# Up products of the recurrent stage as three single-pass products each, on one Trainium2 core

## The reference, cut to what matters

```python
def trunk_layer(x, ...):
    u = rmsnorm(x, g_mix) @ w_in
    u_rw, u_ml, u_pool, u_gate = jnp.split(u, IN_SPLITS, axis=-1)
    o_rw, ... = rwkv7_mix(u_rw, ...)      # 16 heads x 64, recurrent
    o_ml, ... = mlstm_mix(u_ml, ...)
    o_pool, ... = pool_mix(u_pool, ...)
    g = sigmoid(u_gate).reshape(B, L, 3, D_MODEL)
    merged = (g[:, :, 0] * (o_rw @ w_up_rwkv) + g[:, :, 1] * (o_ml @ w_up_mlstm)
              + g[:, :, 2] * (o_pool @ w_up_pool))
    x = x + merged @ w_out
    ...                                    # cross attention, then a mixture of experts
```

## Time and profile before

| | us |
|---|---|
| median of 3 runs (lowest, highest) | 1915.89 (1915.38, 1916.56) |
| the profiled execution, its own time | 1918.07 |
| its span, first to last instruction | 1916.1 |
| PE busy in the span | 1748.7 (91%) |
| DVE, ACT, POOL busy in the span | 910.2, 604.8, 270.5 |
| mean granted TensorE clock (1 is 2.4 GHz) | 0.960 |

### The profile page before, as it was taken

One profiled execution on the slowest core, in us unless ns is written; L12 is line 12 of the kernel. 1 busy time (PEld: TensorE's weight loads), 2 busy tenths in 40 slices (PEclk: granted clock), 3 DMA queues, 4 the chain that ended last, 5 costly groups with the idle time before them and its releaser, 6 DMA issues. The chain is left out here.

```text
span 1916.1 us, 36779 instructions
## 1 busy us (share of the span) xinstructions
PE 1748.7 (91%) x14891; PEld 1439.4 (75%) x14891; DVE 910.2 (48%) x1610; ACT 604.8 (32%) x890; POOL 270.5 (14%) x286
## 2 busy tenths in 40 slices
PE   7999999999999999999998999999898868777675
PEld 7999899998787778778777999999796434443242
DVE  6553445555756676576665445455423222121223
ACT  5243223333443344344335333335432101110012
POOL 0550003112010100100010000850050000000002
PEclk9999999999999999999998999999998988898888
DMA  7445353434232223233215446455638999999995
GB/s 270 174 155 187 110 179 117 173 135 167 100 112 90 99 101 122 87 112 112 90 55 204 155 175 250 152 220 214 238 159 338 422 431 432 431 431 431 431 431 248
DMA packets 46600, 408.98 MB, mean 213 GB/s; under 512 B 6580, under 2 KB 8376, under 8 KB 16696
## 3 DMA queue, kind: packets, MB, share of 16 engines
q1 hardware_dynamic: 46520, 407.81, 54.2%
HBM read 396.62 MB, written 11.18 MB: 213 GB/s over the span
## 5 line engine op out<-in xcount | busy, mean ns | idle before, releaser
L387 PE MATMUL ps<-x_high,w_high 128*128 128x288 f32 x928 | 257.4, 303 | 9.3 <-ACT w_high L593 9.3
L388 PE MATMUL ps<-x_rest,w_high 128*128 128x288 f32 x928 | 253.1, 299 | 0.0
L387 PEld LDWEIGHTS ps<-x_high,w_high 128*128 128x128 f32 x928 | 177.1, 191 | 12.8 <-ACT w_high L593 10.2
L388 PEld LDWEIGHTS ps<-x_rest,w_high 128*128 128x128 f32 x928 | 177.1, 191 | 0.5
L549 ACT ACTIVATE w_high<-w_raw 128x2048 fp32r<-128x2048 f32 x57 | 109.2, 1915 | 153.9 <-DMA w_raw<-in_w_main 77.5
L1101 PE MATMUL ps<-x_high,r_high 128*128 128x288 f32 x512 | 145.8, 308 | 3.8 <-ACT r_high L1352 3.8
L660 DVE TENSOR_TENSOR w_rest<-w_raw,w_high 128x2048 fp32r<-128x2048 f32 x58 | 137.1, 2369 | 11.0 <-ACT w_high L549 11.0
L2557 PE MATMUL ps<-half_a,xg 128*32 128x512 f32 x240 | 81.4, 840 | 62.3 <-DMA half_b<-in_w_egu 62.0
L1101 PE MATMUL ps<-rx_low,r_high 128*128 128x288 f32 x480 | 134.7, 305 | 0.0
L392 PE MATMUL ps<-x_high,w_rest 128*128 128x288 f32 x928 | 132.1, 295 | 1.0 <-DVE w_rest L660 1.0
L392 PEld LDWEIGHTS ps<-x_high,w_rest 128*128 128x128 f32 x928 | 126.0, 188 | 1.2 <-DVE w_rest L660 1.2
(11 more groups left out here) (600 smaller groups left out, 3824.1 us busy)
## 6 DMA issues: line engine op xcount, KB each, us to landing
w_raw<-in_w_main SPq DMA_DIRECT2D x57, 1024.0 KB, 4.8
ring<-in_w_g SPq DMA_DIRECT2D x32, 1024.0 KB, 4.8
half_a<-in_w_egu SPq DMA_DIRECT2D x15, 2048.0 KB, 18.0
half_b<-in_w_egu SPq DMA_DIRECT2D x15, 2048.0 KB, 22.3
ring<-in_w_u SPq DMA_DIRECT2D x32, 512.0 KB, 4.2
ring<-in_w_gate SPq DMA_DIRECT2D x8, 2048.0 KB, 7.8
ring<-in_w_out SPq DMA_DIRECT2D x8, 2048.0 KB, 7.8
half_d<-in_w_egu SPq DMA_DIRECT2D x8, 2048.0 KB, 20.7
```

Source lines behind the costliest of these rows:

```text
L387: mm(o, high[:, t % 2, k, :], x_h[:, k, :], start=(k == 0), stop=False)
L388: ins = mm(o, high[:, t % 2, k, :], x_l[:, k, :], start=False, stop=False)
```

## The change

1. The up products become three single-pass products each, like the gates: up group product numbers run to 24. Products 0 to 15 are high weights by high and low inputs, 16 to 23 the weights' rests by the high inputs. ACT makes the high part of an up tile (`up`, step `j..`, 128x1024, into one buffer `up_high`), POOL its rests (`rest`, step `r..`, 128x1024, into the tile's place). PE waits for `j..` ahead of product 0 and for `r..` ahead of product 16. `j..` waits until the tile before has been read by PE (step `V..`) and by POOL. For `U01`, `U10`, `U11` both are made in the same lap, for `U00` at the end of the lap before.
2. `o_ml` and `o_pool` are split once, in the front stage: ACT rounds (`outcome_high`, and a second scaled copy of the pooling outputs), POOL subtracts (`outcome_rest`, and one operation over all of `o_pool`). The first up tile is split there too, at the stage's end. DVE does `o3` ahead of the last tile's evacuation, and the last tile's rest earlier.
3. The fillers are laid anew. ACT's second half of `split("11")` moves from the fourth level to behind `sas` (with a wait on PE in `G11`, step `i11`), DVE's second half of `rest("11")` behind `s0`. SP waits for `l11` too ahead of one load in the last lap.
4. The last lap of ACT and POOL is written out behind the loop, since it has no tile for a next lap. `bc` moves into another tensor; the scratch for descriptors shrinks from 1024 to 256.

```diff
--- before.py
+++ after.py
+            with ExitStack() as split:
+                sb("o_room", [P, 2 * KH, T], split)
+                o_h, o_l = rounded("o_high", [P, 2 * KH, T], "o_room"), rounded("o_rest", [P, 2 * KH, T], "o_ml")
+                with ExitStack() as c:
+                    front = sb("front", [P, FRONT], c)
+                    up_h, up_rest = rounded("up_high", [P, KH, P], "front"), rounded("up_rest", [P, 2, KH, P], "ring", 6144)
+                    stage_front(nc, ctx, A, O, locals())
+                stage_rwkv(nc, ctx, A, O, locals())
...
+            def outcome_high(h):
+                act.wait_ge(*((g_.sem, g_.at(f"o{h}")) if h < MLH - 1 else (v.sem, v.at("o3"))))
+                fn(o_h[:, 2 * h:2 * h + 2, :], o_ml[:, 2 * h:2 * h + 2, :], ACT.Copy).then_inc(o_high, 1)
...
-                        ins = fn(o_pool[:, 2 * h + e, :], ps[:, 4 + e, 0:T], ACT.Copy, scale=par("pool_scale", 2 * h + e))
+                        by = par("pool_scale", 2 * h + e)
+                        fn(o_pool[:, 2 * h + e, :], ps[:, 4 + e, 0:T], ACT.Copy, scale=by)
+                        ins = fn(o_h[:, KH + 2 * h + e, :], ps[:, 4 + e, 0:T], ACT.Copy, scale=by)
...
+                if h >= 2:
+                    outcome_high(h - 2)
...
+            outcome_high(MLH - 2)
+            outcome_high(MLH - 1)
+            act.wait_ge(env["up_slots"][0], 16)
+            act.wait_ge(q.sem, q.at(f"dB{MLH - 1}"))
+            fn(up_h[:, :, :], up_raw, ACT.Copy).then_inc(up_high, 1)
...
-                step(t + 7)
+                if h < MLH - 1:
+                    step(t + 7)
+            rest(TILES - 1)
             inverse_of(MLH - 1)
-            evacuate(TILES - 1)
+            evacuate(TILES - 2)
             dve.wait_ge(g_.sem, g_.at(f"y{MLH - 1}"))
             dve.wait_ge(v.sem, v.at(f"rs{MLH - 1}"))
             v.done(finish(tt, MLH - 1), "o3")
+            evacuate(TILES - 1)
 
         @block.gpsimd
...
+            tt(o_l[:, KH:2 * KH, :], o_pool[:, :, :], o_h[:, KH:2 * KH, :], ALU.subtract)
...
+            def outcome_rest(h):
+                pool.wait_ge(o_high, h + 1)
+                tt(o_l[:, 2 * h:2 * h + 2, :], o_ml[:, 2 * h:2 * h + 2, :], o_h[:, 2 * h:2 * h + 2, :], ALU.subtract)
...
+                if h:
+                    outcome_rest(h - 1)
             gated(MLH - 1)
+            outcome_rest(MLH - 2)
+            outcome_rest(MLH - 1)
+            pool.wait_ge(up_high, 1)
+            tt(up_rest[:, 0, :, :], up_raw, up_h[:, :, :], ALU.subtract)
...
+            sp.wait_ge(v.sem, v.at("l11", N - 1))
...
                     if kind == "U":
+                        of = i - 1 if name == "U00" else i
                         if lo == 0:
-                            pe.wait_ge(up_slots[b], i * 32 + 16 * d + 16)
+                            pe.wait_ge(a.sem, a.at("j" + name[1:], of))
                             pe.wait_ge(v.sem, v.at(f"m1{b}", i - 1) if d == 0 else v.at(("wm0", "su1")[b], i))
+                        o = ps[:, (1, 7)[b], 0:T]
                         for t in range(lo, hi):
-                            src = (o_ml, o_pool)[b]
-                            ins = mm(ps[:, (1, 7)[b], 0:T], w_up[:, b, t, :], src[:, t, :], start=(t == 0), stop=(t == KH - 1))
-                        if hi == KH:
+                            k = t // 2 if t < 2 * KH else t - 2 * KH
+                            if t < 2 * KH:
+                                ins = mm(o, up_h[:, k, :], (o_h, o_l)[t % 2][:, KH * b + k, :], start=(t == 0), stop=False)
+                                if t == 2 * KH - 1:
+                                    q.done(ins, "V" + name[1:])
+                                continue
+                            if k == 0:
+                                pe.wait_ge(g_.sem, g_.at("r" + name[1:], of))
+                            ins = mm(o, up_rest[:, b, k, :], o_h[:, KH * b + k, :], start=False, stop=(k == KH - 1))
+                        if hi == 3 * KH:
                             q.done(ins, name)
                         return
                     o = ps[:, 6 if name == "G01" else 0, 0:T]
...
+                        if name == "G11" and t == KD:
+                            pe.wait_ge(a.sem, a.at("i11", i))
...
-                filler("U00", 0, 8)
-                filler("U01", 0, 4)
+                filler("U00", 0, 24)
+                filler("U01", 0, 20)
...
                 filler("G00", 0, 48)
-                filler("U01", 4, 8)
+                filler("U01", 20, 24)
                 filler("G01", 0, 48)
...
                 filler("G10", 17, 22)
                 back(1)
-                filler("G10", 22, 32)
+                filler("G10", 22, 31)
                 forward(2)
-                filler("U10", 0, 2)
+                filler("U10", 0, 7)
                 back(2)
                 sample("sz0", lambda h: sxm[:, 0, h, :], lambda h: ident_s)
-                filler("U10", 2, 4)
+                filler("U10", 7, 14)
                 forward(3)
-                filler("U10", 4, 6)
+                filler("U10", 14, 16)
+                filler("G10", 31, 36)
                 back(3)
                 sample("sz1", lambda h: sxm[:, 1, h, :], lambda h: st_[:, h, :])
-                filler("U10", 6, 8)
+                filler("G10", 36, 43)
                 forward(4)
-                filler("G10", 32, 40)
+                filler("G10", 43, 48)
+                filler("U10", 16, 18)
                 back(4)
                 sample("su1", lambda h: sz[:, h, :], lambda h: su[:, h, :])
-                filler("G10", 40, 48)
+                filler("U10", 18, 24)
...
                 q.done(ins, "z5")
-                filler("U11", 0, 2)
+                filler("U11", 0, 6)
...
                 q.done(ins, "u5")
-                filler("U11", 2, 4)
+                filler("U11", 6, 12)
                 q.done(ins, "z6")
-                filler("U11", 4, 6)
+                filler("U11", 12, 18)
                 q.done(ins, "u6")
-                filler("U11", 6, 8)
+                filler("U11", 18, 24)
...
+            def turn(i, last=False):
...
+                def up(name, of):
+                    n = order.index(name)
+                    act.wait_ge(up_slots[n % 2], of * 32 + 16 * (n // 2) + 16)
+                    act.wait_ge(q.sem, q.at("V" + order[n - 1], i))
+                    act.wait_ge(g_.sem, g_.at("r" + order[n - 1], i - 1 if n == 1 else i))
+                    a.done(fn(up_h[:, :, :], w_up[:, n % 2, :, :], ACT.Copy), "j" + name)
...
+                up("01", i)
                 split("00")
...
                 split("10")
+                up("10", i)
...
-                        split("11", 8, 16)
+                        up("11", i)
...
                 a.done(fn(tok[upper, 2, 0:P], ps[upper, 5, P:2 * P], ACT.Copy, scale=-1.0), "sas")
+                split("11", 8, 16)
                 act.wait_ge(q.sem, q.at("g1", i))
...
+                if last:
+                    a.left_out(act, "j00", i)
+                else:
+                    up("00", i + 1)
...
-                rest("11", 8, 16)
                 WQ("s0")
                 halves = [slice(64 * h, 64 * h + 64) for h in H]
                 for o in halves:
                     ins = ts(st0[o, o], ps[o, 2, 0:64], er[o, P - 1:P], ec[o, 1:2], ALU.mult, ALU.mult)
                 v.done(ins, "s0")
+                rest("11", 8, 16)
                 WQ("s1")
...
+                def rest(name):
+                    b = int(name[1])
+                    g_.done(tt(up_rest[:, b, :, :], w_up[:, b, :, :], up_h[:, :, :], ALU.subtract), "r" + name)
+                pool.wait_ge(a.sem, a.at("j01", i))
+                rest("01")
...
+                pool.wait_ge(a.sem, a.at("j10", i))
+                rest("10")
                 pool.wait_ge(v.sem, v.at("m01", i))
                 m = mrg[:, bass.ds(i * 2, 1), :].rearrange("p o t -> p (o t)")
                 g_.done(tt(m, m, gtmp[:, :], ALU.add), "m0")
+                pool.wait_ge(a.sem, a.at("j11", i))
+                rest("11")
                 pool.wait_ge(a.sem, a.at("sas", i))
                 g_.done(spread(vnx[:, :, :], tok[0:2 * NSM, 2, 0:P]), "nx")
+                if last:
+                    g_.left_out(pool, "r00", i)
+                else:
+                    pool.wait_ge(a.sem, a.at("j00", i))
+                    rest("00")
                 pool.wait_ge(v.sem, v.at("m11", i))
                 m = mrg[:, bass.ds(i * 2 + 1, 1), :].rearrange("p o t -> p (o t)")
```

More of the change, by code:

```diff
@@ L212, in stage_front @@
         SUM_AFTER, SLOTS = 4, 3
-        x_h, x_l = env["x_h"], env["x_l"]
+        x_h, x_l, o_h, o_l, up_h, up_rest = (env[n] for n in "x_h x_l o_h o_l up_h up_rest".split())
         raw, w_rest = placed("w_raw", [P, SLOTS, KD, P], "ring"), rounded("w_rest", [P, SLOTS, KD, P], "ring")
@@ L247, in stage_front @@
         whole = ring[:, :, :].rearrange("p s n -> p (s n)")
+        up_raw = whole[:, 6144:7168].rearrange("p (k n) -> p k n", n=P)
```

(26 more changed lines are left out.)

16 lines of the change are left out of this document (8 added, 8 removed).

## The result

| | before | changed |
|---|---|---|
| median of 4 runs (lowest, highest) | 1916.22 (1915.38, 1918.37) | 1943.49 (1942.70, 1947.57) |
| profiled execution's span | 1916.1 | 1940.5 |
| PE, DVE, ACT, POOL busy | 1748.7, 910.2, 604.8, 270.5 | 1741.6, 929.4, 641.9, 358.0 |

The ratio is 1.014 (95% interval 1.0125 to 1.0154): the change makes the kernel 27.3 us slower; the two profiled spans differ by 24.4. Forecast were 16 us (1932, range 1920 to 1946). Direction and range hold; against the 24.4 of the spans the size is short by a third, against the 27.3 of the medians by more. The rest of the text looks for that third, and tests the waits that made up the sum.

A forecast was written before the change was run, and what follows sets the result against it. PE's own work was taken to bound the recurrent lap; 2.80 less work against new waits summed to +1.84 a lap, +14.7 in eight, +16.0 with the front: 1932, range 1920 to 1946.

The forecast's parts named there:

- PE's work: 32 up products a lap, each 0.3975 as three single-pass products for 0.485 in float32: 2.80 us less per lap.
- U01's high part and o: Lap's head: PE waits 1.60 for ACT's up_high; POOL's r01 (2.1) delays DVE's o, so z starts 1.55 later.
- the 0.61: PE's wait for the rests of G00 in the kernel before; forecast to stay.
- The port: DVE with two SBUF inputs and POOL reading SBUF exclude each other; without the rule z starts 0.24 sooner each lap.
- G01 and G10: PE asks for these gates' rests before DVE has them: new waits of 0.84 at G01, 1.65 at G10's third level.
- z6: Shorter fillers bring PE to z6 before DVE's u5: new wait 0.6, up to 1.0 if POOL takes 2.56.
- What costs nothing: ACT's and POOL's other new work, moved split and rest halves, and DMAs are covered; failing, a few tenths a lap.
- The front: Front stage's end: behind o3 ACT rounds and POOL subtracts last outcomes and first up tile, +1.3 once.
- The sum: Per lap -2.80 + 1.55 + 0.84 + 1.65 + 0.60 = +1.84; eight laps +14.7; with the front +16.0.
- The rival that the waits move along: DVE's chains come sooner with PE, so G01, G10 and z6 don't wait: 1907; faster cases have chance 0.13.
- The clock: Rival: PE's longest waits, 1.60 and 1.65, lower its clock, 1.6 more a lap, 1945; chance 0.15, shared with POOL hold-ups.

The follow-up runs named there:

- f1_small_r01: e1_g10 with POOL's r01 cut from 1024 columns to 8, some products computed with wrong weights; ratio 1.0016, lap 67.5 against 67.8.
- f3_halves_r11: e1_g10 with ACT's loop turned, r01 in two halves under DVE's reciprocals, and r11 only behind DVE's us_r; ratio 0.994, repeated 0.9963, lap 65.75.
- e3_free_rounding: The changed kernel without the stage's rounding of up tiles by ACT and POOL, PE's order kept, wrong weights; ratio 1.0156, lap 67.3 at full clock.
- e4_before_g10_early: The kernel before with only G10's rests asked for early, at the third level ahead of back(3); ratio 1.0059.
- e1_g10: The changed kernel with G10's rests asked for only behind back(3) at the third level; ratio 1.0028, median 1925.1.

## Why the prediction was right in direction and short in size

**PE's work, -2.80 a lap: right.** With the rests late and the rounding free the lap is 67.37 - 65.7 = 1.7 shorter, and `G01`'s wait (0.76 there) takes most of the other 1.1.

**U01's high part and o: right in kind, short by 0.58 at `z`, and even again at `G00` by luck.** PE had `up_high` 5.13 into the lap, 0.35 later than taken. POOL's 128x1024 took 2.35 to 2.48; I took 2.1, nearer to the row with 64 partitions, and the other row's 2.56 was the closer one. The Trainium skill gives 4.50 us for 2048 float32 columns ("GPSIMD Engine Reference", section "3.1 Elementwise"), by which an estimate for half of it is 2.25, also closer than 2.1. `z` started 8.33 into the lap (696.28 - 687.95), 2.13 later than before and not 1.55: PE had four products of `U01` left when `r01` ended, at 7.55 and not at 7.2, and was through with them only after `o`, which was ready at 7.86. But the slip did not last: at `G00`'s rests PE was 1.52 late, since the 0.61, which "stays" in the prediction, was taken up. So 1.52 stands for the sum's 1.55 because two errors cancel.

**The port: right.** POOL's subtraction stops DVE's two-input operations in SBUF, `o`, `y` or `dx_r`, whichever it meets, and not the reciprocals, which read one tensor. This agrees with the rule of the Trainium skill that the prediction cites. The prediction priced the case without it at only 0.24 less a lap. No run has `r01` without the port; `f1_small_r01`, almost without `r01`, gave 0.3, since PE's own lateness stands beside it.

**G01 and G10: right; z6: right in number only.** 0.84, 1.65 and 0.6 were forecast, 0.88, 1.33 and 0.78 measured. For `z6` the fillers' shortness was given as the cause; `f3_halves_r11` shows it to be POOL's `r11` holding up `dx_r` (1.40 for 0.47, where the prediction had half a microsecond and took it to be absorbed). `e3_free_rounding`, with the same short fillers and no `r11`, has no wait there.

**What costs nothing: right** for the laps. The eight laps cost 1.3 more than 8 x 2.03. Most of it lies in the first lap: against the kernel before, the way to the first `z` is 2.3 longer (PE waits 2.00 there for `up_high`), the first stretch 3.0, the next five together 10.1, the last 1.3 and the rest of the last lap 0.8, at full clock.

**The front, +1.3: 0.8 measured.**

**The sum, +1.84 a lap: 2.03**, and with the first lap's head 17.5 in eight for 14.7. That is 2.8 of the missing 8.4 us; the front and what lies behind the stage give 0.8 back.

**The rival that the waits move along: refuted.** Even with the rounding free (`e3_free_rounding`), the waits at `G01` and `G10` stand, at 0.76 and 1.35, so it is DVE's own order that sets them.

**The clock: the step that failed.** It stood as a rival at 0.15, with a loss of 1.57 in each lap (12.6 in eight) and 1945 as its time. It came, though not in each lap: four falls, 6.4 us in the profiled execution, the largest part of what was missing. The 1943.5 lie above the forecast's own 1922 to 1940 and in the range only because that was drawn out for this rival; without the 6.4 they would be 1937. I compared only the lengths of the waits, 1.60 and 1.65, with the 1.50 after which the clock had stayed. The wait that did it was 1.33 long (1.11 in `e4_before_g10_early`), and the longer one at the head did nothing. What counts is not that length alone. At the third level PE's small products and short pieces of fillers leave it busy for 2.02 of 3.30 us; but about the head's wait it was busy for 1.84 of 3.40 (`e1_g10`, 680.00 to 683.40) without a fall. What sets the two places apart stays open, as does why only some laps fall: that was not tried.

## What to carry to other kernels

When a product on a bound engine becomes cheaper, look up what that engine will ask for sooner, and who makes it: with 2.8 us less in a lap and no rounding to do, the lap was 0.1 shorter in the new filler order, and 1.7 shorter once `G10`'s rests were asked for later. Two things that are late side by side must be taken away together; each experiment on one of them will seem to acquit it. And a subtraction on POOL belongs under a DVE instruction that reads one tensor or PSUM: under `r01`'s halves the reciprocals kept their 1.95, and under `r11` in `f3_halves_r11` DVE's product with a PSUM input (L1566) kept its 0.46.

## What the hardware showed that I had not expected

- A fall of TensorE's clock (to 1.2 GHz) followed a wait of 1.11 to 1.35 us, in two to six of the eight laps of the kernels that had it at the third level, and in other laps in another execution; it made a lap 0.6 to 4.0 us longer. It never followed the wait of 1.56 at the lap's head.
- A table load of 1.28 stands at the start of ACT's loop body, ahead of a copy that does without it in straight-line code. Turning the loop moved it under a wait, and `up_high` came 1.3 sooner.
